# mLSTM recurrence: the products that spread the maximum and decay rows, 8 rows of the array against 128 zero-padded rows

## What is computed

```python
b = jnp.cumsum(lf, axis=-1)
d_log = jnp.where(tril, b[..., :, None] - b[..., None, :] + ig[..., None, :], -jnp.inf)
inter = b + m_st[..., None]
m_t = jnp.maximum(inter, jnp.max(d_log, axis=-1))
s = jnp.einsum('bhtd,bhsd->bhts', q, k) * jnp.exp(d_log - m_t[..., None])
w_inter = jnp.exp(inter - m_t)
num = (jnp.einsum('bhts,bhsv->bhtv', s, v)
       + w_inter[..., None] * jnp.einsum('bhvd,bhtd->bhtv', c_st, q))
den = jnp.sum(s, axis=-1) + w_inter * jnp.einsum('bhd,bhtd->bht', n_st, q)
h = num / jnp.maximum(jnp.abs(den), jnp.exp(-m_t))[..., None]
```

## Time and profile before

| | us |
|---|---|
| median of 3 runs (3246.66 to 3250.02) | 3249.83 |
| the profiled execution | 3242.0 |
| span of its instructions | 3240.2 |
| TensorE busy in the span | 2914.4 (90%) |
| VectorE busy | 1276.7 (39%) |
| ScalarE busy | 574.1 (18%) |
| GpSimd busy | 344.2 (11%) |
| mean granted TensorE clock | 0.937 of 2.4 GHz |

### The profile page before, as it was taken

The page is one execution under the profiler, slowest core; times in us unless marked ns, Lnnn a source line. Parts: engine busy times, 40 slices in busy tenths (PEclk is TensorE's granted clock), DMA queues, the critical chain, the costliest instruction groups (busy, mean ns, idle before and its releaser), DMA issues. The chain is left out here.

```text
span 3240.2 us, 42425 instructions
## 1 busy us (share of the span) xinstructions
PE 2914.4 (90%) x17496; PEld 2234.8 (69%) x17496; DVE 1276.7 (39%) x2182; ACT 574.1 (18%) x1424; POOL 344.2 (11%) x486
## 2 busy tenths in 40 slices
PE   7999789899999999999999898889987958888883
PEld 5877665677777788888888787777876845455541
DVE  5644548322224543434343563553424431111114
ACT  3222128300000200000001332331011101111111
POOL 1012310000000000000000001451011101111112
PEclk8985899999999999999999999998998969999996
DMA  3100020111112111111113320001111169999994
GB/s 126 52 14 1 26 97 30 40 49 41 51 42 98 40 52 41 58 45 52 39 66 91 54 40 14 2 2 50 43 29 76 72 253 408 416 414 409 401 373 196
DMA packets 127056, 356.82 MB, mean 110 GB/s; under 512 B 14088, under 2 KB 58376, under 8 KB 109456
## 3 DMA queue, kind: packets, MB, share of 16 engines
q1 hardware_dynamic: 114912, 336.32, 28.6%
q0 software_dynamic: 10512, 16.80, 1.4%
q10 hardware_dynamic: 1440, 0.99, 0.1%
HBM read 343.18 MB, written 31.46 MB: 116 GB/s over the span
## 5 line engine op out<-in xcount | busy, mean ns | idle before, releaser
L454 PE MATMUL banks<-hT_upper,split_weights 128*128 128x512 f32 x2304 | 745.7, 400 | 14.3 <-PEq L204 8.2
L454 PEld LDWEIGHTS banks<-hT_upper,split_weights 128*128 128x128 f32 x2304 | 435.4, 189 | 116.7 <-issue 21.8
L445 PE MATMUL banks<-split_weights,hT_upper 128*128 128x512 f32 x1536 | 483.8, 396 | 23.0 <-DVE hT_lower L137 9.9
L454 PE MATMUL banks<-hT_lower,split_weights 128*128 128x512 f32 x1152 | 451.0, 391 | 0.0
L445 PEld LDWEIGHTS banks<-split_weights,hT_upper 128*128 128x128 f32 x1536 | 291.6, 191 | 86.3 <-issue 19.1
L445 PE MATMUL banks<-split_weights,uT_upper 128*128 128x512 f32 x1024 | 315.6, 389 | 0.0
L445 PE MATMUL banks<-split_weights,hT_lower 128*128 128x512 f32 x768 | 303.4, 395 | 0.0
L2949 PE MATMUL banks<-expert,ex_xT 128*64 128x256 f32 (+1 forms) x1632 | 260.1, 394 | 46.4 <-DMA expert<-in_w_up 21.8
L454 PEld LDWEIGHTS banks<-hT_lower,split_weights 128*128 128x128 f32 x1152 | 217.9, 189 | 55.1 <-issue 11.2
L2949 PEld LDWEIGHTS banks<-expert,ex_xT 128*64 128x64 f32 (+1 forms) x1632 | 169.9, 148 | 100.9 <-issue 59.2
L445 PEld LDWEIGHTS banks<-split_weights,uT_upper 128*128 128x128 f32 x1024 | 191.9, 188 | 39.6
(11 more groups left out here) (476 smaller groups left out, 3695.6 us busy)
## 6 DMA issues: line engine op xcount, KB each, us to landing
expert<-in_w_gate SPq DMA_DIRECT2D x51, 1024.0 KB, 14.2
expert<-in_w_up SPq DMA_DIRECT2D x51, 1024.0 KB, 21.6
expert<-in_w_down SPq DMA_DIRECT2D x51, 1024.0 KB, 24.8
raw_weights<-in_w_in SPq DMA_DIRECT2D x38, 1024.0 KB, 5.4
raw_weights<-in_w_up SPq DMA_DIRECT2D x16, 1024.0 KB, 5.3
raw_weights<-in_w_down SPq DMA_DIRECT2D x16, 1024.0 KB, 5.0
hT<-in_w_gate SPq DMA_DIRECT2D x13, 1024.0 KB
hT<-in_w_up SPq DMA_DIRECT2D x13, 1024.0 KB
```

What stands on the lines that cost most here:

```text
L445: last = pe.matmul(bank, acts[x][:, r * KT // 2 + k, m * P:(m + 1) * P].bitcast(F32R), w[y][:, k, :].bitcast(F32R), start=(r == 0 and k == ...
L454: last = pe.matmul(out, w[x][:, k, c0:c0 + P].bitcast(F32R), acts[y][:, k, t0:t0 + nt].bitcast(F32R), start=(k == 0 and x == y), stop=(k = ...
```

## The change

The row M gets 128 partitions (it was 8), and the place of W is taken with all its 128 partitions; GpSimd sets both to zero at the start of `mlstm_inputs`, and VectorE waits for that before it writes the 8 rows of M. The constant `pick8` becomes 128 x 8 x 128 with rows 8 to 127 zero, and so grows from 32 KB to 512 KB. `m_rows` and `decays` take all 128 rows of both operands. The decay columns keep 8 rows.

```diff
+        zeroed = c.sem(mem, "in1_rows_zeroed")
...
+        @block.gpsimd
+        def _(pl):
+            for r in (M, W):
+                nc.gpsimd.memset(row(r, padded=True), 0.0).then_inc(zeroed, 1)
...
+            dve.wait_ge(zeroed, 2)
             s_dve.then_wait(dve, nc.vector.scalar_tensor_tensor(row(M), row(X), c.k["dir8"][:, 3:4], row(T1), ALU.mult, ALU.add))
...
-                    last = nc.tensor.matmul(c.bank(0)[:, h * P:(h + 1) * P], c.k["pick8"][:, 4 * d + h, :], row(M)[:, chunk(j)],
+                    last = nc.tensor.matmul(c.bank(0)[:, h * P:(h + 1) * P], c.k["pick8"][:, 4 * d + h, :], row(M, padded=True)[:, chunk(j)],
                                             start=True, stop=True)
...
-                                                row(W)[:, chunk(j)], start=True, stop=True)
+                                                row(W, padded=True)[:, chunk(j)], start=True, stop=True)
...
-                        last = nc.tensor.matmul(c.psum[half_rows, 5, (2 * d + i) * TT:(2 * d + i + 1) * TT], c.k["pick8"][:, 4 * d + h, 0:M_QK],
+                        last = nc.tensor.matmul(c.psum[half_rows, 5, (2 * d + i) * TT:(2 * d + i + 1) * TT], c.k["pick8"][0:8, 4 * d + h, 0:M_QK],
                                                 dec_row, start=True, stop=True)
...
-                    ("pick8", [8, 8, P]), ("dir8", [8, 4]), ("b_if", [8, 2]),
+                    ("pick8", [P, 8, P]), ("dir8", [8, 4]), ("b_if", [8, 2]),
...
-                m_row = c.sb(ml, "ml_m_row", [8, S])
+                m_row = c.sb(ml, "ml_m_row", [P, S])
...
-                def row(i):
-
+                def row(i, padded=False):
+
+                    if padded:
+                        return m_row[:, :] if i == 5 else hcT[:, 0, :]
                     if i == 5:
-                        return m_row[:, :]
+                        return m_row[0:8, :]
...
-    pick = np.zeros((8, 8, P), np.float32)
+    pick = np.zeros((P, 8, P), np.float32)
```

## The result

| | before | after |
|---|---|---|
| median | 3248.24 us (4 runs, 3244.72 to 3250.02) | 3200.29 us (4 runs, 3198.44 to 3201.95) |
| ratio after to before | | 0.9853, 95% interval 0.9839 to 0.9868 |
| the profiled execution | 3242.0 | 3200.82 |
| its span | 3240.2 | 3199.1 |
| mean granted clock | 0.937 | 0.954 |

The change gives 48 us, 1.5%.

A forecast was written before the change was run, and what follows sets the result against it. TensorE, always busy but mostly at half clock in the mLSTM stage, was taken as the bound. Terms of -39.3 and +1.4 gave -37.9 us: 3204.1 for the profiled execution, 3211.9 for the median; range 3203 to 3226.

The forecast's parts named there:

- What bounds the stage, and why rows matter: mLSTM stage: TensorE always busy, mostly at half clock; 8-row products precede clock falls, so 128 rows should hold full clock.
- (a): Padded maximum and decay products in the mLSTM stage: same count and columns, so cost 0.
- (b): Units 0 to 13 of the mLSTM stage: full clock takes 105.6 us to 67.9, gain 37.7.
- (c): Second half of the stage: ScalarE's order holds units 9 to 12 to about 5.3 us each, 1.1 us back.
- (d): End of the stage, TensorE's last two units up to the last copy: 2.7 us saved.
- (e): Front: pick8 at 512 KB, queued ahead of the fourth x tile, costs 1.4 us; bounds 0 and 5.2.
- (f): Two GpSimd memsets, 2.5 us in all, and VectorE's wait ahead of L573: hidden, cost 0.
- the same difference gives 3211.9: Last step: the median's 7.8 us above the profiled execution, added to 3204.1 for the changed kernel.
- an early rise: Start of the stage, work ahead of 207 us: up to 1.5 us more gain if the clock rises within it.
- Half-way: Rival: the clock rises but still falls in part of the stage; half the gain, 3231.6 us, chance 0.12.
- no effect: Rival: zero rows or filling don't move the stage's clock; 3251.2 us, up to 3255, chance 0.10.
- The other side: Rival: 128-row loads of L710 and L721 can't overlap products; 3289 us, or 3231 at full clock, chance 0.03.

## Why the prediction was right or wrong

- **What bounds the stage, and why rows matter: right.** TensorE's own pace was the path, and the granted clock set that pace. The padding of the products moved it, and the preparation without it did not (147.6 us). The objection I had noted, half clock through 64- and 128-row products, is still not explained.
- **(a) "Cost 0": wrong by sign.** The padded products are cheaper: the period at full clock is 4.85 instead of 5.03 us. I compared L721 with L785 and L710 with L797, at half clock for the latter, and had no row for a whole unit with both padded. The gain hangs on L717 alone (4.85 with the maximum alone padded, 5.03 with the decays alone). Over the units this is the larger part of the 2.3 us by which (b) and (c) came out short.
- **(b) and (c).** -36.6 forecast, -38.9 measured. ScalarE's L824 does become late in the second half, as said, but every other period: 5.42, 4.94, 5.42, 4.95 us instead of four of 5.3.
- **(d) The end: right,** 2.65 against 2.7 us.
- **(e) The constant: mechanism right, size off:** 1.0 instead of 1.4 us up to L493, and behind that hidden in the 3 us of scatter of the stage's start.
- **(f) Right in effect.** The memset of W took 2.03 us, not 1.3, and VectorE's cast beside it 1.57 instead of 1.23 us; nobody waited.

```profile
42.39 0.95 POOL L549 MEMSET ml_m_row<- 128x1024 f32 x1 [5.02 <-POOLq L220]
42.85 1.57 DVE L133 CAST split_weights<-raw_weights 128x2048 fp32r<-128x2048 f32 x1 [0.74 <-PEq L220]
43.29 2.03 POOL L549 MEMSET x<- 128x1024 f32 x1
```

- **The step that failed: "the same difference gives 3211.9".** I took the 7.8 us by which the median of before stood above its profiled execution as a property of measuring, and added them to the changed kernel. They were largely the clock's luck in the very stage that the change mends: 27 us of full clock in the traced stage, 17 in the next trace, which made 8.2 of the 12.9 us between those two; no execution right at the median was traced. The changed kernel has no such scatter in the stage, and its median stands 0.5 us below its profile, not 7.8 above. That is 8.3 of the 11.6 us between forecast and result, 3.3 are the terms above. From 3204.1, the forecast for the profiled execution, the result of 3200.3 would have been 4 us away, inside the same range moved down by the 7.8 us (3195 to 3218).
- **The range's lower end and the scatter.** The two bounds named for 3205, an early rise (1.5 us) and no (e) (1.4 us), give 3209.0 and not 3205. And 6.5 us as what a measurement can tell was too little for the kernel before, whose 21 executions span 15.7 us; three runs 3.4 us apart had hidden that.
- **The rivals.** "Half-way" and "no effect" fell; rows that are all zero were enough to bring the clock. "The other side" fell too: the padded L717 got shorter, 1.06 instead of 1.15 us, with 128-row loads. It had been put too strongly: the 8-row products all lie in the same eight rows, so by that rival's own rule the loads between them had nothing to lose. The two rules of the Trainium skill (TensorE: Matmul & The Clock Gate): that unbroken work brings the full clock ("Why this matters for your kernels") does not hold with 8-row products, 10.00 of 10.00 us busy at 0.50 in the kernel with the preparation alone; that loads overlap only across row groups (Part 3, "The mechanism") may hold or not, no run here tells, but it put no cost on the padded kernel. The same page (Part 1, "What's actually happening") says that the gate looks at time in a rhythm of its own that does not start anew with the kernel; this would explain the luck, and no run here shows it.

## What to carry to other kernels

Read the granted clock beside the busy time: a stage in which TensorE never pauses can still run at 1.2 GHz, and its price is the whole stage's pace, here 9.05 against 5.03 us a unit. If part of its products use few rows of the array, try padding those rows with zeros: here the zeros cost no time in the stage and 1.0 us at the front, where they were loaded, and padding one of two such products was enough. And before a profiled execution is tied to a median, ask whether the stage that the change touches is the one that scatters: if it is, the offset goes with it.

## What I had not expected of the hardware

- Rows that are zero in both operands are enough to keep the clock up (stage 94.5 us, clock 1.00 with 120 zero rows of 128).
- For these products in this stage: 8 rows 0.54 to 0.61 granted over the stage, 16 rows 128.5 us with the clock lost after 240 us, 32 and 64 rows 99.6 us with the clock held (one execution each but for 8).
- Behind the 128-row L804, the eight records of L717 take 0.98 to 0.99 us up to the start of L728 with 128 rows, and 1.08 to 1.09 with 8, 32 or 64, at full clock.
- An unchanged kernel scattered over 16 us (21 executions, 3239.9 to 3255.6) while the padded one stayed within 3.5 us (five), on a single core.
